# One block of an RWKV-7 scan: a product moved to GpSimd, a small solve laid over four array quarters, and two ScalarE steps swapped

## What is computed

```
    S_t = S_{t-1} diag(w_t) + (S_{t-1} a_t) b_t^T + v_t k_t^T ; y_t = S_t r_t.
    def step(state, inp):
        r_t, w_t, k_t, v_t, a_t, b_t = inp
        sa = jnp.einsum('bhij,bhj->bhi', state, a_t)
        state = (state * w_t[:, :, None, :]
                 + sa[..., :, None] * b_t[..., None, :]
                 + v_t[..., :, None] * k_t[..., None, :])
        y = jnp.einsum('bhij,bhj->bhi', state, r_t)
        return state, y
```

## Time and profile before

| | us |
|---|---|
| median of 3 runs | 2629.35 |
| lowest and highest | 2628.88 and 2630.71 |
| the profiled execution's own time | 2628.31 |
| its span in the trace | 2626.6 |
| mean granted TensorE clock | 0.988 of full speed |
| busy in the span: TensorE, VectorE, ScalarE, GpSimd | 97%, 58%, 44%, 18% |

### The profile page before, as it was taken

The page is one execution under the profiler, slowest core; times in us unless marked ns, Lnnn a source line. Parts: engine busy times, 40 slices in busy tenths (PEclk is TensorE's granted clock), DMA queues, the critical chain, the costliest instruction groups (busy, mean ns, idle before and its releaser), DMA issues.

```text
span 2626.6 us, 74898 instructions
## 1 busy us (share of the span) xinstructions
PE 2547.5 (97%) x30741; PEld 2102.5 (80%) x30741; DVE 1520.5 (58%) x3199; ACT 1163.3 (44%) x2626; POOL 484.0 (18%) x622
## 2 busy tenths in 40 slices
PE   6999999999999999999999999999999999999995
PEld 6777777777778888888888888888888888888883
DVE  2412121212157677777767777776677777667774
ACT  3324242323225455544445554454455445445542
POOL 3210101010121112211211121121112112111210
PEclk8999999999999999999999999999999999999997
DMA  8632322323210001000000101000010100001000
GB/s 338 255 112 81 110 93 99 102 90 112 81 65 10 26 29 39 26 34 26 26 26 26 42 26 34 26 26 26 26 42 26 34 26 26 26 26 42 26 18 25
DMA packets 68706, 153.08 MB, mean 58 GB/s; under 512 B 3977, under 2 KB 37342, under 8 KB 66398
## 3 DMA queue, kind: packets, MB, share of 16 engines
q1 hardware_dynamic: 63134, 130.08, 14.1%
q0 software_dynamic: 1680, 11.01, 1.0%
q10 hardware_dynamic: 3632, 7.87, 0.8%
HBM read 98.61 MB, written 50.33 MB: 57 GB/s over the span
## 4 chain that ended last, share of the span: by engine, by line
PE 74%; DVE 16%; ACT 4%; issue 3%; DMA 1%; DVEq 0%; SPq 0%; ACTq 0%
PE banks L949 20%; PE banks L355 16%; PE banks L984 9%; PE banks L387 8%; PE banks L932 7%; PE banks L1004 6%; DVE SM L1587 2%; DVE LA L1570 2%; DVE LA L1576 2%; PE banks L960 1%; PE banks L1112 1%; DVE t L1467 1%; DVE mix L1438 1%; DVE kk L1474 1%; DVE stmp L1519 1%
## 5 line engine op out<-in xcount | busy, mean ns | idle before, releaser
L949 PE MATMUL banks<-xT,w 128*128 128x128 f32 x5232 | 634.0, 279 | 0.0
L949 PEld LDWEIGHTS banks<-xT,w 128*128 128x128 f32 x5232 | 598.3, 192 | 31.1 <-issue 27.1
L1255 ACT ACTIVATE LX<-banks 128x512 f32<-128x512 f32 (+1 forms) x384 | 184.9, 524 | 642.6 <-DVE WT L1532 436.5
L355 PE MATMUL banks<-xT,w 128*128 128x256 f32 x2048 | 448.3, 381 | 4.8 <-ACT xT L475 4.8
L355 PEld LDWEIGHTS banks<-xT,w 128*128 128x128 f32 x2048 | 391.3, 191 | 65.3 <-issue 10.5
L932 PE MATMUL banks<-xT,w 128*64 128x128 f32 x6944 | 420.1, 274 | 0.0
L932 PEld LDWEIGHTS banks<-xT,w 128*64 128x64 f32 x6944 | 380.3, 137 | 6.3
L984 PE MATMUL banks<-wo,Y 128*128 128x512 f32 x512 | 234.3, 601 | 4.7 <-DVE Y L1492 4.7
L387 PE MATMUL banks<-wo,yc 128*128 128x512 f32 x512 | 224.8, 592 | 0.0
L672 DVE TENSOR_SCALAR gate<-gate 128x1024 f32<-128x1024 f32 x16 | 11.1, 694 | 367.7 <-ACT gate L495 367.7
L1532 DVE TENSOR_TENSOR WT<-banks,level_mask 128x256 f32<-128x256 f32 x256 | 102.6, 422 | 187.7 <-PE banks L1004 179.7
(11 more groups left out here) (185 smaller groups left out, 3587.6 us busy)
## 6 DMA issues: line engine op xcount, KB each, us to landing
x_in<-in_x SPq DMA_DIRECT2D x16, 1024.0 KB, 7.4
xr<-in_x SPq DMA_DIRECT2D x32, 512.0 KB, 4.3
xt_dram<-xT SPq DMA_DIRECT2D x32, 512.0 KB, 8.6
h_dram<-xr SPq DMA_DIRECT2D x32, 512.0 KB, 2.6
xT<-xt_dram SPq DMA_DIRECT2D x32, 512.0 KB, 3.3
gate_row<-h_dram SPq DMA_DIRECT2D x32, 512.0 KB, 4.3
out<-gate_row SPq DMA_DIRECT2D x32, 512.0 KB, 2.6
w<-in_w_in POOLq DMA_DIRECT2D x8, 1088.0 KB, 10.9
```

The costliest lines, as they stand in the source:

```text
L355: last = nc.tensor.matmul(bank[t // 2][:, (t % 2) * T1:(t % 2 + 1) * T1], w1[:, k, t * P:(t + 1) * P], xT[:, k, :], start=(k == 0), stop=( ...
L949: last = (by_halves if halves else nc.tensor.matmul)(bank[b][:, q * P:(q + 1) * P], w2[:, k, (t0 + q) * P:(t0 + q + 1) * P], xT[par][:, k, :],
L1255: s(nc.scalar.activation(to, of, ACT.Copy), lx_ready, hold=False)
```

## The change

Four edits: the reads product of block n + 1 is formed by GpSimd at the end of its `head`, behind the BK products, and TensorE waits for it before the Gram matmuls; `take_u(0)` comes ahead of `exp_low_rank(0)` on ScalarE; `solve` uses all four quarters of the array, for which `from_state` writes the pairs with odd p to swapped halves, AI is laid out to match by twice as many VectorE instructions of half the size, and the result lands in two banks; `solve(1)` also waits for `take_y(0)`.

```
 # tensor
-    last = nc.tensor.matmul(bank[5][half(e), p * HD:(p + 1) * HD], LA[e][:, p, j, 0], SV[e][:, p],
+    last = nc.tensor.matmul(bank[5][half(e ^ p % 2), p * HD:(p + 1) * HD], LA[e][:, p, j, 0], SV[e][:, p],
                             start=True, stop=True)
 def solve(j):
     s.wait(r_ready, j + 1)
+    if j:
+        s.wait(y_ready, j)
     let_through(pe, pe_gate)
-    for p in range(NP):
-        for e in range(2):
-            h = half(e)
-            last = nc.tensor.matmul(bank[5][h, 256 + p * HD:256 + (p + 1) * HD], LX[h, p // 2, j, p % 2, 0], R[h, p], start=True, stop=True)
+    for a in range(2):
+        for r, c in QUARTERS:
+            x = r ^ c
+            last = nc.tensor.matmul(step_banks[1][half(c), x, 256 + a * HD:256 + (a + 1) * HD], LX[half(r), a, j, x, 0],
+                                    R[half(r), 2 * a + x], start=True, stop=True)
 # front, ahead of the Gram matmuls
     s.wait(lhs_ready, 1)
+    s.wait(read_ready, 1)
 # scalar
+def update_of(e):
+    return step_banks[1][half(e), :, 256:256 + 2 * HD].rearrange("p x (a t) -> p x a t", a=2)
-    s(nc.scalar.activation(UV[j][0][half(0), :, :].rearrange(flat), bank[5][half(0), 256:512], ACT.Copy), act_half, hold=False)
+    s(nc.scalar.activation(UV[j][0][half(0), :, :].rearrange("p (a x) t -> p x a t", x=2), update_of(0), ACT.Copy), act_half, hold=False)
...
+    take_u(0)
     if ahead:
         exp_low_rank(0)
-    take_u(0)
-    if ahead:
         exp_low_rank(1)
 # gpsimd, end of head(n)
+    if not first:
+        s.wait(y_ps, NC)
+    hd.wait(exps_ready, 2)
+    for e in range(2):
+        h = half(e)
+        hd(nc.gpsimd.tensor_tensor(LA[e][h, :, :, 1], chunks(mix[h, 0:4]), chunks(sig[h, 0]), ALU.mult),
+           read_ready if e else head_pool)
 # vector
-    s.wait(exps_ready, 2)
-    for e in range(2):
-        h = half(e)
-        s(nc.vector.tensor_tensor(LA[e][h, :, :, 1], chunks(mix[h, 0:4]), chunks(sig[h, 0]), ALU.mult), hold=False)
...
-    s(nc.vector.tensor_tensor(AI[h, :, j, :, 0], SM[j][e][h, :, 0].rearrange("q (a p) t -> q a p t", a=2),
-                              ident64[h, :].unsqueeze(1).unsqueeze(1).broadcast_to([HD, 2, 2, HD]), ALU.add),
-      hold=bool(e and j))
+    for x in range(2):
+        s(nc.vector.tensor_tensor(AI[half(e ^ x), :, j, x, 0], SM[j][e][h, :, 0].rearrange("q (a x) t -> q a x t", a=2)[:, :, x],
+                                  ident64[h, :].unsqueeze(1).broadcast_to([HD, 2, HD]), ALU.add),
+          hold=bool(e and j and x))
```

More of the change, by code:

```diff
@@ L62 @@
 HEAD_DVE = 9
-DVE_OWN = 14
+DVE_OWN = 16
 LN_MAX = 1e19
@@ L787, in second_pass @@
             head_dve = signal("head_dve", HEAD_DVE)
-            head_pool = signal("head_pool", 1)
+            head_pool = signal("head_pool", 2)
+            read_ready = signal("read_ready", 1)
             dve_own = signal("dve2_own", DVE_OWN)
@@ L1255, in take_step @@
                         s(nc.scalar.activation(to, of, ACT.Copy), lx_ready, hold=False)
+                def update_of(e):
+                    return step_banks[1][half(e), :, 256:256 + 2 * HD].rearrange("p x (a t) -> p x a t", a=2)
                 def take_u(j):
                     s.wait(u_ps, j + 1)
-                    s(nc.scalar.activation(UV[j][0][half(0), :, :].rearrange(flat), bank[5][half(0), 256:512], ACT.Copy), act_half, hold=False)
-                    s(nc.scalar.activation(UV[j][1][half(1), :, :].rearrange(flat), bank[5][half(1), 256:512], ACT.Copy), u_ready)
+                    s(nc.scalar.activation(UV[j][0][half(0), :, :].rearrange("p (a x) t -> p x a t", x=2), update_of(0), ACT.Copy), act_half, hold=False)
+                    s(nc.scalar.activation(UV[j][1][half(1), :, :].rearrange("p (a x) t -> p x a t", x=2), update_of(1), ACT.Copy), u_ready)
                 def second_values(to):
@@ L1363, in ones_of, with head @@
                     return ones[part, :].unsqueeze(1).broadcast_to([HD, NP, HD])
-                def head(n):
+                def head(n, first=False):
                     hd.block(n)
@@ L1418, in gpsimd @@
                 pool.wait_ge(zero_ready, 1)
-                head(0)
+                head(0, True)
                 each_block(pool, run)
```

## The result

The changed kernel is slower: 2657.7 us (median of 4 runs, 2654.4 to 2661.7) against 2629.2, a ratio of 1.0111 [1.0099, 1.0123]. The forecast was 2644 in a range of 2608 to 2662, with 0.66 on slower. The sign and the main mechanism held; the loss is 28.5 us where 15 were forecast.

What follows compares the result with a forecast made beforehand. Bound: TensorE to the key norm, then a serial ScalarE and VectorE chain. -0.37 - 1.44 + 1.83 + 0.52 = +0.54 us per block, 31 blocks +16.7, less 1.5 outside: 2644 us; own range 2637 to 2652, wider 2608 to 2662.

Steps and rivals of the forecast that it cites:

- The sign: Whole kernel: slower than before by more than 0.2% (5.3 us), chance 0.66.
- the main mechanism: VectorE's serial chain: GpSimd's two reads products take turns with VectorE's two-SBUF-input instructions, costing VectorE +1.83 us per block.
- The bound: Per block: TensorE's work up to the key norm, plus one serial ScalarE and VectorE chain from 1738.5 to 1760.2.
- Reads: Reads product moved from VectorE to GpSimd: -1.44 us per block saved, +1.83 paid in turns with GpSimd.
- Rival A: Reads hidden on GpSimd without holding VectorE: about 1.0 us per block faster, 31 us, 2598; chance 0.15.
- B: Rival: only one of the two GpSimd products meets VectorE, -0.36 us per block, 2618 us; chance 0.12.
- Solve and update: Step 0 to key norm: first solve 0.30 us shorter, earlier update closes a 0.07 us gap; -0.37 per block.
- AI: VectorE's AI as eight instructions of 128 elements: 1.13 us per chunk against 0.87, +0.52 us per block.
- rival C: Solve gives nothing, or AI costs nearer its upper bound: +0.9 us per block, 2657 us; chance 0.13.
- Outside the loop: Block 0's reads product off VectorE and the last block's two shorter solves: -1.5 us together.

Runs made afterwards that it cites:

- e4: Kernel before with the update first and the solve in four quarters by output half, AI unchanged, ScalarE copying the result in four pieces: 2623.4 us.
- e3: Changed kernel with GpSimd's two reads products replaced by zero fills that read nothing: 2608.4 us, 0.9919.
- e1: Changed kernel with the reads product back on VectorE: 2645.7 us, 1.0063.
- e2: Kernel before with only the reads product moved to GpSimd, and TensorE's wait for it: 2642.4 us, 1.0052.
- e5: Kernel before with only the update taken ahead of the first exponentials on ScalarE: 2622.3 us, 0.9974.
- e6: Changed kernel with the update behind the first exponentials again: 2667.5 us, 1.0145.
- e12: Kernel before with the update first and only the first of two solves in four quarters, with four small ScalarE copies behind it: 2617.0 us, 0.9956.
- e7: Kernel before with AI formed by eight VectorE instructions of 128 elements instead of four of 256, pairs on the same half: 2642.9 us, 1.0048.
- e10: Changed kernel with AI instructions reordered so that the pairs writing the same half of the partitions stand together: 2659.1 us, 1.0108.
- e13: Kernel before with eight AI instructions that stay in their own partitions, each on the other half than the one ahead: 2657.0 us, 1.0105.
- e11: Kernel before with one of the two reads products (head 1 of each pair) on GpSimd, the other on VectorE: 2635.5 us, 1.0025.

## Why the prediction came out as it did

**The bound, right.** A block is TensorE's work to the key norm and a serial chain behind it. Most differences lie in the part that the edit touches. The exceptions are the +0.12 of the changed kernel, e4's third part, and e3, where VectorE is early enough that TensorE takes the Gram matmuls without a wait; there the last part is 7.98 us and not 8.54.

**Reads, right in size.** Forecast -1.44 + 1.83 = +0.39, measured +0.38 (e1, e2). Line 1475's counterpart took 1.65 us, as forecast. Rival A fell: VectorE isn't left alone beside GpSimd's products (e3 shows what it would have won). B fell too: both products took their turn.

**Solve and update, -0.37 forecast, -0.48 and then +0.12 measured.** The solve's 16 records take 0.39 us in the chain and not 0.31, so it gave 0.22 and not 0.30: half the records of line 1007 take more than half of its 0.62. Why wasn't tested. The update gave 0.26 and not 0.07 (e5), because I read the wait from the gap alone and not from the long first state matmuls behind it. That the shorter solve is worth nothing without the earlier update held (e6).

The +0.12 I had not priced. VectorE's new state (tile SV, lines 1519 and 1525 before) is needed by `from_state(1)`, and VectorE has other work ahead of it that the change doesn't move. In all thirteen profiles the state is done 34.9 us after step 0. The kernel before has step 0 at 1702.80, and the changed one at 1663.91:

```profile
1736.83 0.87 DVE L1525 TENSOR_TENSOR SV<-stmp,dend 64x256 f32<-64x256 f32 x2
1738.20 0.68 PE L1034 MATMUL banks<-SV,LA 128*64 128x64 f32 x16
```

```profile
1697.93 0.87 DVE L1540 TENSOR_TENSOR SV<-stmp,dend 64x256 f32<-64x256 f32 x2
1698.95 0.69 PE L1036 MATMUL banks<-SV,LA 128*64 128x64 f32 x16
```

`from_state(1)` started 0.50 us behind the state and starts 0.15 behind it now, as it does in e4 and e12. So it could come only some 0.35 us earlier, whatever TensorE had won. VectorE's decay sum, which comes behind it, starts 1.03 us after rn where it was 0.90, and at kk 0.36 of the 0.48 is left. The forecast's -0.37 for this part is met by luck: one term was too large, the other too small, and the limit was not in it. The limit is read from the starts; no run moves the state.

**AI, the step that failed.** "I take the row of that size" put +0.52 a block; it is +0.73. The row, line 1485, has the right size but works on all 128 partitions each time: each of its instructions lasts 0.34 us, and the next starts 0.26 us after it, so they overlap. The changed AI's last 0.29 and go from half to half, 0.32 apart (e7, e10, e13). A chunk takes 1.24 us and not 1.13. The row to take was AI itself: 2 x 0.42 us of work in 0.87, no overlap, against line 1549's 2 x 0.42 in 0.76. This is the direction of rival C, but C had +0.9 a block and the block is +0.76; that the time is C's 2657 is chance, made up by what lies outside the loop.

**Outside the loop.** I had -1.5 us for block 0 and the end. In the profiled execution block 0 costs 5.3 us in place of that: 2.3 ahead of its step 0 and 3.0 behind it, and 2.7 of it is the clock (below). The end costs 0.8 and not -0.6. Of the 33.4 us by which its span is longer, the blocks at 0.76 are 23.6, block 0 is 5.3 and the end 0.8. Another 2.0 lie in the first pass, where the lower clock lasts 3.4 us longer than in the kernel before. 1.4 lie in the last two intervals, with VectorE's late pause (0.75 us) and 3.4 us of the lower clock from 2532.5. 0.3 are left over. The median is 4.0 us below this execution and the others weren't profiled, so what of the 28.5 us belongs to which of these isn't known to better than a few us.

## What to carry to other kernels

Before work is moved to an idle GpSimd, look at what VectorE does at that time: if its instructions read two SBUF operands, price the move by turns (here 0.9 us of VectorE for each 1.28 us product), not by GpSimd's share. Making a result's producer shorter was worth nothing while its consumer's queue stood in the way (e6), and moving the result ahead in that queue was worth 7 us by itself (e5): do that first. Then look at what else the next step waits for, since another engine's fixed time can end the gain. When an instruction is cut up, take its price from a row of the same size that also moves over the partitions in the same way, and order the pieces so that neighbours stay on the same ones. And where an operand's place costs an engine that is the bound, see whether the output's place can carry the layout to one that has room.

## What the runs showed of the hardware that was not expected

VectorE's pitch by partitions: four 64x128 instructions of 0.28 us take 1.01 us if they come in pairs that read and write the same half, 1.24 if neighbours don't share it (e7, e13).

TensorE's clock in block 0. There the AI instructions meet GpSimd's copies of the same block. Four take 1.69 and 2.65 us in its two chunks, where two took 1.29 in each, and TensorE waits 3.33 us for the first factor, where it waited 1.51. From 791.7, within that wait, its granted clock is down for 6.8 us. The row of 792 to 800 us of the changed kernel, columns as in the earlier trace rows (clock third from the end), then of the kernel before:

```profile
792.00:800.00 8.00, 7.34 (x80) 6.92 (x84) 2.49 (x8) 2.33 (x5) 0.00 (x0) 0.59 0.00 0
```

```profile
792.00:800.00 8.00, 8.00 (x116) 7.39 (x114) 4.51 (x12) 3.72 (x9) 0.00 (x0) 1.00 0.01 2
```

0.59 is a mixture of the lower level, 1.2 GHz, and the full one. Step 0 takes 1.99 us in place of 1.10, and the portion of the projection behind it 4.79 in place of 2.94:

```profile
792.66 1.99 PE L1006 MATMUL banks<-AI,W 64*64 64x128 f32 x32 [3.33 <-DVE W L1559]
794.57 4.79 PE L951 MATMUL banks<-xT,w 128*128 128x128 f32 x24
```

That is 2.7 us that no instruction count shows. All seven profiled kernels with eight AI instructions (after, e1, e3, e6, e7, e10, e13) have a lowered clock there, and the six with four (before, e2, e4, e5, e11, e12) have 1.00. It goes with the longer wait, 2.6 to 3.4 us in the seven and 1.5 in the six. But the length of one wait doesn't decide it: the waits of 1.1 us in the loop left the clock at 1.00, and so did one of 1.22 us at the end of e6's loop (until 2540.22), while in e10 the clock was at the lower level for 3.4 us from 2530.7, 0.7 us behind a wait of 1.21. What the chip responds to isn't settled here.
